# A hybrid decoder step on one Trainium2 core: who multiplies x by rstd at the head of a layer

## The reference

```
h    = rmsnorm(x, norm_w)              # x * rsqrt(mean(x*x) + EPS) * norm_w
proj = h @ w_in                        # 1024 -> 5648, split over three branches
x    = x + concat(SSD, retention, pooling) @ w_out      # 2048 -> 1024
```

## Time and profile before

| | us |
|---|---|
| median of 3 runs (lowest, highest) | 982.21 (980.66, 984.82) |
| the profiled execution | 985.22 |
| its span, first to last instruction | 983.3 |
| TensorE busy | 947.8 |
| VectorE busy | 692.0 |
| ScalarE busy | 419.6 |
| GpSimd busy | 44.3 |

### The profile page before, as it was taken

One profiled execution on the slowest core, in us unless ns is written; L12 is line 12 of the kernel. 1 busy time (PEld: TensorE's weight loads), 2 busy tenths in 40 slices (PEclk: granted clock), 3 DMA queues, 4 the chain that ended last, 5 costly groups with the idle time before them and its releaser, 6 DMA issues.

```text
span 983.3 us, 18751 instructions
## 1 busy us (share of the span) xinstructions
PE 947.8 (96%) x7934; PEld 905.7 (92%) x7934; DVE 692.0 (70%) x942; ACT 419.6 (43%) x703; POOL 44.3 (5%) x148
## 2 busy tenths in 40 slices
PE   5899999999999999999999999999999999999996
PEld 5799999999998889999999999999989987899995
DVE  5789677867795578674548967777679748686545
ACT  5432354334685226533334225532367632544222
POOL 0000001110010000000000001111101000000000
PEclk9999999999999999999999999998999999999999
DMA  6233322225235444422434242221432452552222
GB/s 263 81 127 102 107 65 66 71 66 176 104 83 172 151 150 142 169 88 65 146 113 145 86 141 65 65 66 50 151 107 87 133 207 65 215 191 78 86 65 97
DMA packets 38277, 113.33 MB, mean 115 GB/s; under 512 B 11088, under 2 KB 13776, under 8 KB 36784
## 3 DMA queue, kind: packets, MB, share of 16 engines
q1 hardware_dynamic: 37936, 111.23, 34.6%
q0 software_dynamic: 256, 0.88, 0.3%
HBM read 94.63 MB, written 17.47 MB: 114 GB/s over the span
## 4 chain that ended last, share of the span: by engine, by line
PE 82%; DVE 9%; ACT 5%; issue 1%; DMA 1%; SPq 0%; DVEq 0%; ACTq 0%
PE acc L530 24%; PE acc L532 23%; PE acc L531 23%; DVE w_lo L1142 2%; ACT w_hi L878 2%; DVE h L1375 2%; PE misc L634 1%; ACT decay L965 1%; PE misc L620 1%; PE misc L728 1%; PE misc L687 1%; DVE h L1365 1%; PE misc L709 1%; PE acc L777 1%; ACT decay L972 1%
## 5 line engine op out<-in xcount | busy, mean ns | idle before, releaser
L530 PE MATMUL acc<-hin,w_hi 128*128 128x288 f32 x1568 | 471.6, 301 | 1.7 <-DVE w_lo L1142 0.9
L531 PE MATMUL acc<-hin,w_hi 128*128 128x288 f32 x1568 | 463.4, 296 | 0.0
L532 PE MATMUL acc<-hin,w_lo 128*128 128x288 f32 x1568 | 463.3, 295 | 0.0
L530 PEld LDWEIGHTS acc<-hin,w_hi 128*128 128x128 f32 x1568 | 295.8, 189 | 15.1 <-issue 11.9
L878 ACT ACTIVATE w_hi<-w_raw 128x1024 fp32r<-128x1024 f32 x122 | 128.8, 1056 | 395.2 <-PE acc L532 393.4
L531 PEld LDWEIGHTS acc<-hin,w_hi 128*128 128x128 f32 x1568 | 296.0, 189 | 0.4
L532 PEld LDWEIGHTS acc<-hin,w_lo 128*128 128x128 f32 x1568 | 295.7, 189 | 0.0
L1142 DVE TENSOR_TENSOR w_lo<-w_raw,w_hi 128x1024 fp32r<-128x1024 f32 x122 | 148.9, 1220 | 139.6 <-ACT w_hi L878 139.2
L530 PE MATMUL acc<-mix,w_hi 128*128 128x288 f32 x384 | 115.7, 301 | 18.3 <-DVE w_lo L1142 12.1
L531 PE MATMUL acc<-mix,w_hi 128*128 128x288 f32 x384 | 114.1, 297 | 0.0
L532 PE MATMUL acc<-mix,w_lo 128*128 128x288 f32 x384 | 114.1, 297 | 0.0
(11 more groups left out here) (210 smaller groups left out, 1036.3 us busy)
## 6 DMA issues: line engine op xcount, KB each, us to landing
w_raw<-in_w SPq DMA_DIRECT2D x122, 512.0 KB, 3.6
decay<-cum_rows SPq DMA_DIRECT2D x8, 1024.0 KB, 5.8
h<-in_ssm SPq DMA_DIRECT2D x16, 512.0 KB, 5.9
out_ssm_s<-h SPq DMA_DIRECT2D x16, 512.0 KB, 7.0
x<-in_x SPq DMA_DIRECT2D x8, 576.0 KB, 6.2
x_kept<-x SPq DMA_DIRECT2D x4, 576.0 KB, 5.4
x<-x_kept SPq DMA_DIRECT2D x4, 576.0 KB, 6.4
out_y<-x SPq DMA_DIRECT2D x8, 288.0 KB, 2.3
```

The source lines that it names most:

```text
L530: pe.matmul(out, wh, hi, start=k == 0, stop=False)
L531: pe.matmul(out, wh, lo, start=False, stop=False)
L532: return pe.matmul(out, wl, hi, start=False, stop=k == KT - 1)
```

## The change

GpSimd multiplies each slice of x by rstd in place, as the first thing in its loop over the layers, after waiting for rstd and, in layer 1, for the stores of x. norm_w now comes in as the scale of ScalarE's cast and as the scalar of VectorE's subtraction, which becomes (x * norm_w) - high part in one instruction. VectorE's scalings go, and so does its wait for the stores.

```diff
@@ ScalarE, beside units 0 to 2
-    go(act(hin[:, 0, j, :], x[:, j, :], ACT.Copy), h_hi, j + 1)
+    go(act(hin[:, 0, j, :], x[:, j, :], ACT.Copy, scale=vec[:, V_NW + j:V_NW + j + 1]), h_hi, j + 1)
@@ VectorE
 def scaled(first, end):
-    for j in range(first, end + 1):
-        if j < end:
-            if l and j == 0:
-                eng.wait_ge(*of(x_out, 64, l - 1))
-            go(V.scalar_tensor_tensor(out=x[:, j, :], in0=x[:, j, :], scalar=v_(V_NW + j),
-                                      in1=rstd[:, :], op0=ALU.mult, op1=ALU.mult), h_full, j + 1)
-        if j > first:
-            eng.wait_ge(*of(h_hi, j))
-            go(V.tensor_tensor(hin[:, 1, j - 1, :], x[:, j - 1, :],
-                               hin[:, 0, j - 1, :].bitcast(F32), ALU.subtract), h_lo, j)
+    for j in range(first, end):
+        eng.wait_ge(*of(h_hi, j + 1))
+        go(V.scalar_tensor_tensor(out=hin[:, 1, j, :], in0=x[:, j, :], scalar=v_(V_NW + j),
+                                  in1=hin[:, 0, j, :].bitcast(F32), op0=ALU.mult, op1=ALU.subtract),
+           h_lo, j + 1)
@@ GpSimd
 for l in range(DEPTH):
+    eng.wait_ge(*of(n_rstd, 1))
+    if l:
+        eng.wait_ge(*of(x_out, 64, l - 1))
+    for j in range(KT):
+        go(G.tensor_tensor(x[:, j, :], x[:, j, :], rstd[:, :], ALU.mult), h_full, j + 1)
     eng.wait_ge(*of(proj, EARLY))
     go(G.memset(rS[:, :, :], 0.0), r_zero, 1)
```

## The result

The change costs time. Fourteen executions of the changed kernel have a median of 987.41 us (986.42 to 990.22), fourteen of the kernel before, timed beside them, 983.05 (980.50 to 985.44): ratio 1.0045, 95% interval 1.0034 to 1.0055, about 4.4 us. The forecast had the direction and the mechanism, and twice the size (+9.0). It drew its lines at 0.5% and gave slower 0.65 and same 0.32: the ratio lies just inside the line and its interval reaches over it, so that the kernel is slower is shown, and that it is slower by 0.5% is not.

A forecast was written before the change was run, and what follows sets the result against it. TensorE, busy 96% of the span, bounds the kernel, so only its waits at the two layer heads matter. Layer 1 +4.4, layer 0 +2.5 and clock +2.1 make +9.0 us: 991.2 us, range 981 to 999.

The forecast's parts named there:

- the mechanism: Both heads: GpSimd multiplies alternate with VectorE's split and subtractions, one instruction at a time; +9.0 us with the clock, chance 0.50.
- The first rival: Both heads: VectorE never waits for GpSimd; layer 0 -0.8, layer 1 +0.6, together -0.2 us, 982.0; chance 0.25.
- the second: Both heads: GpSimd keeps the port through all eight multiplies; +7.5, +6.5 and two clock losses, +18.2 us, 1000.4; chance 0.15.
- the third: Both heads: a multiply costs 0.67 us like a copy and nothing collides; -2.0 us, 980.2; chance 0.05.
- the signs named: Heads: multiplies 1.2 to 1.4 us apart alone, 2.0 to 2.5 beside VectorE; layer 1's unit 3 3 to 5 later; clock below 1.
- The price of a pair: Both heads: a multiply of 1.15 us plus 0.1 for two hand-overs, 1.25, alternating with a VectorE subtraction or split.
- The estimate of 1.26: GpSimd multiply: skill's 4497 ns for a two-input add over 2048 columns, scaled by proportion; would make the sum 1.8 us larger.
- the figure from the copy rows: GpSimd multiply of 576 elements: 0.19 us fixed plus two read passes of 0.48, so 1.15 us; bounds 0.67 and 1.63.
- +2.5 forecast: Layer 0: turns delay the split and VectorE's reads, so unit 4 starts at 48.8 instead of 46.37.
- +6.5 forecast with the clock: Layer 1: unit 4 4.4 us later by turns (528.6 instead of 524.19), plus 2.1 for TensorE's slowed clock.
- 4.4 + 2.5 + 2.1: Whole kernel: layer 1's lateness, layer 0's lateness and the clock's loss added up to +9.0 us.
- The term that was mis-sized: Turns in both heads: unit 4 later by 2.5 us in layer 0 and 4.4 in layer 1.

The follow-up runs named there:

- dummy multiplies: Kernel before, plus eight GpSimd multiplies of rstd by rstd at each head into memory nobody reads: 996.06 us, ratio 1.0137.
- busy wait: Changed kernel, plus 40 unneeded TensorE products before unit 3 of layer 1: 987.09 us, ratio 1.0034 to the kernel before.
- earlier store: Last store of x issued at unit 3 of layer 1 instead of unit 4: 977.09 us on the kernel before, 979.20 on the changed one.
- earlier cast: Store moved up, and layer 0's unit 2 weights cast before rstd: 976.67 and 977.21 us on the kernel before, 979.04 on the changed one.
- dummy writes: Kernel before, plus eight GpSimd fills of 1500 columns at each head, which read nothing: 983.14 us, ratio 1.0005.
- VectorE multiplies: Changed kernel, but VectorE multiplies x by rstd again and norm_w stays in the cast and subtraction: 983.58 us, ratio 1.0001 to the kernel before.

## Why the prediction was right and where it wasn't

**The mechanism was right.** VectorE and GpSimd take turns, one instruction at a time, and both wait: the split at 29.07 is held, a subtraction that is called while a multiply runs (32.76, beside the multiply from 31.88 to 33.80) ends only some 0.6 us behind it, the reads from PSUM pass. This settles what the earlier trace rows had left open: VectorE does stand still behind a GpSimd read. The lock that the Trainium skill states (SBUF — State Buffer, section Who interferes with whom) is so shown in both directions by the dummy multiplies; the turns were not quite whole lengths (next point). The first rival (VectorE never waits) fell with the split, the second (GpSimd keeps the port for all eight) with the turns, the third (cheap, no collision) with 1.43 us. Of the signs named, one came out low: multiplies start 1.9 us apart where a subtraction goes between, not 2.0 to 2.5 (2.4 with a split).

**Turns aren't the whole loss.** A GpSimd multiply is also longer than the scaling that it replaces, 1.43 against 0.8 us, and no run keeps the one without the other. An estimate from the rows of layer 1: three multiplies that never wait end 4.2 us after the landing of the store (1.38 from start to start, 1.43 the last); cast 0.8, weight cast 1.0, split 1.2, read 0.8 and the hand-overs between them put unit 3 at 8.2, where it was at 7.08 and is at 10.56. So about a third of those 3.5 us would be the length and two thirds the turns. In layer 0 the same chain would end at 8.3 behind rstd, before TensorE is through with unit 2 (3.2 + 6.6 = 9.8), so there it would be turns alone.

**The price of a pair: two errors that partly cancelled.** The sum took 1.15 for a multiply and 0.1 for its hand-over. Alone it takes 1.43 us. Only with the same tensor for both inputs does it take 1.14, as in the dummy multiplies. But a pair costs less than the two lengths: multiply and subtraction 1.90 where 1.43 + 0.82 = 2.25; multiply and split 2.4 where 1.43 + 1.22 = 2.65; in the dummy kernel 1.66 where 1.14 + 0.81 = 1.95. So the hand-over is not +0.1 but about -0.3: the end of one instruction lies beside the beginning of the other (neighbours on one engine overlap a little too: the first three multiplies of layer 1 start 1.38 apart and take 1.43). A pair was put at 2.07 and is 1.90; that it came so near was luck, as the multiply was put 0.28 too low and the hand-over 0.4 to 0.45 too high. Six such pairs a head make 1.0 us, most of what VectorE's reads came earlier than forecast. The estimate of 1.26 by proportion from the Trainium skill (GPSIMD Engine Reference, section Elementwise, side by side) was nearer to 1.43 than the figure from the copy rows, and low as well.

**Layer 0: +2.5 forecast, +0.9 traced.** Against the end of rstd, unit 3 starts at 11.62 us (39.72 less 28.10) instead of 10.19 (39.37 less 29.18): +1.4 where +2.0 was forecast, by the shorter pairs. The clock fell in this head too (0.60 over 31.70 to 36.00), where the sum put no loss; it cost nothing, for TensorE, slowed, was through with unit 2 just as VectorE's read ended (38.82 + 0.76 = 39.58; no wait shows before unit 3 at 39.72). Unit 4 starts +1.2 later, and by unit 6 it is +0.9 (31.23 against 30.29): of the lateness, 0.3 had been waited inside unit 4 in the kernel before as well, for the last subtractions, which the sum didn't count.

**Layer 1: +6.5 forecast with the clock, +4.6 traced.** From the landing of the store, unit 3 starts at 10.56 us (519.18 less 508.62) instead of 7.08 (517.25 less 510.17): +3.5, forecast +3.9. The clock fell as expected: 0.50 in unit 3. **One step was wrong as reasoning**, the sum of the two: "4.4 + 2.5 + 2.1" adds the clock's loss to the lateness of VectorE's read. But unit 4 starts at the later of the two; by the prediction's own terms that is TensorE at 527.7 + 2.1 = 529.8, +5.6 and not +6.5. In the run VectorE's read ended at 525.84, by which unit 4 could have started 3.3 us later than before, where 4.4 was forecast; TensorE, slowed, came at 527.65, 5.0 later, and waited for nothing. So the slow clock added 1.7 of the 2.1, and 0.4 of the total was regained by unit 6 (+4.6). **The term that was mis-sized** is the turns: of the 3.5 us by which both heads came earlier than forecast, VectorE's reads make 2.4 (layer 0 +1.2 instead of +2.5, layer 1 +3.3 instead of +4.4), the false sum 0.4, and 0.7 was regained behind unit 4. The busy wait shows the other end: at full clock unit 4 waits for VectorE (0.22) and is +3.4 late.

**What nobody forecast: the clock elsewhere.** The heads together lost 0.9 + 4.6 = 5.5 us, the two profiled executions differ by 1.5. Of the 4.0 between, 1.1 came before the first rstd (28.10 against 29.18), and 12 x (0.86 - 0.72) = 1.7 and 20 x (0.91 - 0.83) = 1.6 are the clock's at the two later windows (4.4 in all, so 0.4 was lost in other places). The mean granted clock of the kernel before differs from run to run as well (0.988 to 0.993, and its time ranges over 5 us), so a pair of traces can't tell whether the change shortens those stretches. The medians differ by 4.4, with an interval of 3.3 to 5.4, against 5.5 by the heads: what is left, about 1 us, stays open.

## What to carry to other kernels

Handing VectorE's work to an idle GpSimd saved nothing here, where both read two inputs from SBUF at the same time: price it as a pair that takes turns, a little under the sum of both lengths, and look for the place where that pair stands in the chain. Count a slower clock and a late producer as the later of the two, not as a sum. And where a long wait for a store or a cast sets the start of such a chain, moving the store can be worth more than moving the arithmetic: here an earlier store gave 5.8 us by one line. Whether it also lowers what the choice of engine costs is not settled by the times (2.1 us with the store alone, 1.8 to 3.9 with the earlier cast as well, 4.4 without either).

## What the runs showed of the hardware that was not expected

- A two-input GpSimd multiply of 576 columns takes 1.43 us with two tensors and 1.14 with one tensor twice, each without VectorE beside it.
- VectorE's wait for GpSimd's reading is booked as busy time: 1358 ns for an instruction of 817.
- The same wait on TensorE had either outcome. A wait of 3.14 us before unit 2 went on at full clock in the kernel before; the same 3.14 in the kernel with dummy writes and 3.51 in the changed kernel were followed by a stretch at half pace. Before unit 3 of layer 1, 2.68 went on at full clock in the kernel before, and 2.53 (dummy writes) and 2.94 (VectorE multiplies) were followed by half pace (0.50 over 517.50 to 520.80 and over 519.30 to 522.60). Waits of 5.38 and 7.52 (dummy multiplies) and 6.26 were followed by half pace each time.
